# One table set for logarithm and exponential, shorter warm runs and a moved product in a two-layer transformer trunk

## What is computed

```python
for layer in range(2):
    mod = silu(c) @ ada_w[layer] + ada_b[layer]
    sh1, sc1, g1, sh2, sc2, g2 = split(mod, 6)
    h = rmsnorm(x, norm_g[layer, 0]) * (1 + sc1) + sh1
    y = diff_attention(h, ...) if layer == 0 else conformer_conv(h, ...)
    x = x + g1 * y
    h = rmsnorm(x, norm_g[layer, 1]) * (1 + sc2) + sh2
    x = x + g2 * conv_ffn(h, ...)
return rmsnorm(x, final_g)

def diff_attention(h, ...):      # per head: two softmaxes, subtracted
    p = softmax(q1 k1 + bias) - lam * softmax(q2 k2 + bias)
    o = rmsnorm(p @ v, subln_g) * (1 - lambda_init)
def conformer_conv(h, ...):
    a = glu(h @ w_pw1 + b); a = causal_dwconv(a, w_dw) + b_dw   # 31 taps
    return silu(layernorm(a)) @ w_pw2 + b_pw2
```

## Time and profile before

| | us |
|---|---|
| median of 3 runs | 1267.98 |
| the 3 runs | 1267.55, 1267.98, 1268.33 |
| the profiled execution, its own time | 1265.96 |
| span of its trace | 1264.2 |
| PE busy in the span | 1231.0 |
| DVE busy | 702.3 |
| ACT busy | 567.5 |
| POOL busy | 540.8 |

### The profile page before, as it was taken

How to read it: one execution, slowest core, us unless ns; L and a number is a source line. 1 busy time by engine, 2 the same in 40 slices (tenths; PEclk the granted TensorE clock), 3 DMA queues, 4 the chain that set the end, 5 groups by cost and what they waited for, 6 DMA issues and landing times.

```text
span 1264.2 us, 16847 instructions
## 1 busy us (share of the span) xinstructions
PE 1231.0 (97%) x5494; PEld 983.4 (78%) x5494; DVE 702.3 (56%) x1157; ACT 567.5 (45%) x899; POOL 540.8 (43%) x273
## 2 busy tenths in 40 slices
PE   7999999989999999999999999999999999999996
PEld 7877777667888888888888776577888888888884
DVE  5667766753766733346887899972533333340002
ACT  4366656644543344442223666762544444442221
POOL 1333322223433444444442699744344444454440
PEclk6899999999999999999998999999999999999998
DMA  9744443222456422236763222113233232232321
GB/s 360 214 151 148 146 154 133 101 100 67 149 184 199 166 90 93 92 105 230 232 244 112 83 84 67 33 34 100 67 100 100 100 100 90 93 106 95 105 78 66
DMA packets 45639, 157.04 MB, mean 124 GB/s; under 512 B 5536, under 2 KB 5792, under 8 KB 45600
## 3 DMA queue, kind: packets, MB, share of 16 engines
q1 hardware_dynamic: 44928, 156.21, 37.0%
q10 hardware_dynamic: 672, 0.34, 0.1%
HBM read 154.10 MB, written 2.42 MB: 124 GB/s over the span
## 4 chain that ended last, share of the span: by engine, by line
PE 81%; DVE 12%; issue 3%; ACT 2%; POOL 1%; DMA 1%; DVEq 0%; SPq 0%; ACTq 0%; POOLq 0%
PE psum L917 24%; PE psum L918 24%; PE psum L919 24%; DVE psum L1754 6%; PE psum L947 2%; PE psum L928 1%; DVE psum L1480 1%; DVE pt_lo L1489 1%; PE psum L951 1%; PE psum L1074 1%; DVE acc L1331 1%; DMA ada_first<-ada_w 1%; POOL acc_p L515 1%; PE psum L1101 1%; PE psum L1113 0%
## 5 line engine op out<-in xcount | busy, mean ns | idle before, releaser
L502 POOL TENSOR_TENSOR w_lo<-w_raw,w_hi 128x1024 fp32r<-128x1024 f32 (+1 forms) x192 | 455.2, 2387 | 670.6 <-ACT w_hi L589 670.6
L917 PE MATMUL psum<-h_hi,w_hi 128*128 128x512 f32 x1152 | 465.9, 404 | 4.1 <-DVE x L1584 2.2
L918 PE MATMUL psum<-h_lo,w_hi 128*128 128x512 f32 x1152 | 452.5, 393 | 0.0
L919 PE MATMUL psum<-h_hi,w_lo 128*128 128x512 f32 x1152 | 452.1, 392 | 0.0
L917 PEld LDWEIGHTS psum<-h_hi,w_hi 128*128 128x128 f32 x1152 | 219.0, 190 | 54.3 <-issue 7.2
L919 PEld LDWEIGHTS psum<-h_hi,w_lo 128*128 128x128 f32 x1152 | 218.5, 190 | 46.9
L918 PEld LDWEIGHTS psum<-h_lo,w_hi 128*128 128x128 f32 x1152 | 218.7, 190 | 45.6 <-issue 3.4
L589 ACT ACTIVATE w_hi<-w_raw 128x1024 fp32r<-128x1024 f32 (+1 forms) x192 | 195.6, 1032 | 82.7 <-DMA w_raw<-w_tiles 82.6
L917 PE MATMUL psum<-a_hi,w_hi 128*128 128x512 f32 x352 | 137.1, 390 | 1.0 <-issue 1.0
L919 PE MATMUL psum<-a_hi,w_lo 128*128 128x512 f32 x352 | 137.0, 389 | 0.0
L918 PE MATMUL psum<-a_lo,w_hi 128*128 128x512 f32 x352 | 136.9, 389 | 0.0
(11 more groups left out here) (185 smaller groups left out, 1342.7 us busy)
## 6 DMA issues: line engine op xcount, KB each, us to landing
w_raw<-w_tiles SPq DMA_DIRECT2D x160, 512.0 KB, 3.4
ada_buf<-ada_w SPq DMA_DIRECT2D x32, 512.0 KB, 3.4
w_raw<-w_tiles SPq DMA_DIRECT2D x32, 448.0 KB, 3.2
ada_late<-ada_w SPq DMA_DIRECT2D x28, 512.0 KB, 5.2
ada_mid<-ada_w SPq DMA_DIRECT2D x20, 512.0 KB, 4.5
ada_first<-ada_w SPq DMA_DIRECT2D x16, 512.0 KB, 10.1
x<-x_in SPq DMA_DIRECT2D x4, 512.0 KB, 7.0
bias<-rel_scratch SPq DMA_DIRECT2D x8, 256.0 KB, 6.1
```

Of the source, the lines that this page charges most:

```text
L502: nc.gpsimd.tensor_tensor(w_lo[:, slot, 0:k], w_raw[:, (ph.tile + l) % 2, 0:k], f(w_hi[:, slot, 0:k]), ALU.subtract).then_inc(lo_done, 1)
L917: nc.tensor.matmul(dst, w_hi[:, slot, k], rhs_hi, start=first, stop=False)
L918: nc.tensor.matmul(dst, w_hi[:, slot, k], rhs_lo, start=False, stop=False)
L919: return nc.tensor.matmul(dst, w_lo[:, slot, k], rhs_hi, start=False, stop=last)
```

## The change

The last of the seven late modulation sums gets its own buffer `acc_last` (in the place of `pad_g`), its product moves from ahead of PW1 to the end of the layer norm's sums, into another PSUM bank, and `late_out` is split in two calls.

```diff
--- before.py
+++ after.py
@@ -86,6 +86,7 @@
 DOWN1 = UP1.after(3, DK)
 HEAD_FROM_2 = Phase(2, 6, 3, HEADS - 2)
 PW1_FROM_2 = Phase(PW1.group + 2, PW1.tile + 4, 2, DK - 2)
+LN_EXP_SET = 6
 LATE0 = 4 + 8 * HEADS
 SQ_ORDER = (4, 5, 0, 1, 2, 3, 6, 7)
 EARLY = 4
@@ -229,7 +230,8 @@
         ada_mid = at("ada_mid", [P, 2, 2, S], F32, a_lo_at + 4 * S * 2 * MID)
         acc_mid = at("acc_mid", [P, S], F32, a_lo_at + 4 * S * (2 * MID + 4))
         ada_late = at("ada_late", [P, 4, 2, S], F32, h_base)
-        acc_late = at("acc_late", [P, LATE, S], F32, h_base + 4 * 2 * S * 4)
+        acc_late = at("acc_late", [P, LATE - 1, S], F32, h_base + 4 * 2 * S * 4)
+        acc_last = at("acc_last", [P, S], F32, offset_of["pad_g"])
 
         cursor[0] = big
         u_pad = sb("u_pad", [P, 2, TAPS - 1 + S])
@@ -255,6 +257,7 @@
         ACC_B, ACC_A, TAPS_PE, SHIFT_AT = 4, 5, 6, 7
         SUM_AT, SQ_AT = 0, 1
         DELTA_AT, RSTD_AT, SILU_AT = 4, 5, 6
+        LAST_OUT = 2
 
 
         params_in, consts_in = sem("params_in"), sem("consts_in")
@@ -598,9 +601,18 @@
                     split_tile(ph, i, ph.per_group * c + j)
 
 
+            def load_ln_exp():
+
+                nc.scalar.add_instruction(mybir.InstLoadActFuncSet(
+                    name=nc.get_next_instruction_name(), engine=mybir.EngineType.Activation,
+                    act_func_set_id=LN_EXP_SET, ins=[], outs=[]))
+
             def load_table(function):
 
-                nc.scalar.activation(sm(TABLE), ones[:, 0:1], function)
+                if function == ACT.Ln:
+                    load_ln_exp()
+                else:
+                    nc.scalar.activation(sm(TABLE), ones[:, 0:1], function)
 
             def inverse_rms(n):
 
@@ -747,7 +759,6 @@
                     copy_v(it, c + 1)
                 for m in range(EARLY if isinstance(it, int) and c == 0 else 0):
                     o_high(m)
-                load_table(ACT.Ln)
                 act.wait_ge(ms_done, lin(it, c + 1, 2))
                 nc.scalar.activation(o_sq[:], psum[:, OB], ACT.Ln, bias=sm(EPS5),
                                      scale=1.0 / (2 * HD)).then_inc(ms_read, 1)
@@ -1196,7 +1207,7 @@
 
             pairs(OUT, None, x_done, 0, 2)
             square_sum(1, 2)
-            keep_warm(18)
+            keep_warm(12)
 
             def late_ada(total, first, n):
 
@@ -1227,11 +1238,14 @@
             def last_ada(q):
 
                 pe.wait_ge(ada_used, 8 * (LATE_CH + q + 1))
-                ada_product(WARM, acc_late[:, q], at_=4 * q)
+                if q < LATE - 1:
+                    ada_product(WARM, acc_late[:, q], at_=4 * q)
+                else:
+                    ada_product(LAST_OUT, acc_last[:])
 
             last_ada(0)
             square_sum(2, 1)
-            for q in range(1, LATE):
+            for q in range(1, LATE - 1):
                 last_ada(q)
 
             def pe_taps(t):
@@ -1286,10 +1300,11 @@
             pe_taps(DK - 1)
             for n in range(4, DK):
                 dev_sums(n)
-            keep_warm(24)
+            last_ada(LATE - 1)
+            keep_warm(16)
             pairs(PW2, 4 * DK, x_done, 2 * DK, 2)
             square_sum(3, 2)
-            keep_warm(18)
+            keep_warm(12)
             pairs(UP1, 5 * DK, act_ready, FM, 1)
             group = down(DOWN1, 1)
             with pe.Fori(1, DOWN1.bodies) as i:
@@ -1400,7 +1415,7 @@
                                                in1=psum[:, OB],
                                                op0=ALU.mult, op1=ALU.mult).then_inc(t_ready, 1)
                     if m > lo:
-                        if n == 2 and m <= LATE:
+                        if n == 2 and m < LATE:
                             dve.wait_ge(ada_mm, LATE_CH + m)
                         dve.wait_ge(h_hi_ready, HI_AT[n] + m)
                         V.scalar_tensor_tensor(out=h_lo[:, m - 1], in0=turn(n, m - 1),
@@ -1605,13 +1620,13 @@
                 ab = prm[:, b4:b4 + 4] if isinstance(n, int) else prm[:, bass.ds(b4, 4)]
                 V.tensor_tensor(to, psum[:, 4, 0:4], ab, ALU.add).then_inc(sc_read, 1)
 
-            def late_out():
-
-                dve.wait_ge(ada_mm, LATE_CH + LATE)
-                first, b = 4 * LATE_CH, PARAMS["ada_b"] + 4 * LATE_CH
-                V.tensor_tensor(mod[:, first:first + 4 * LATE], psum[:, WARM, 0:4 * LATE], prm[:, b:b + 4 * LATE],
+            def late_out(lo, hi, sums):
+
+                dve.wait_ge(ada_mm, LATE_CH + hi)
+                first, b = 4 * LATE_CH + 4 * lo, PARAMS["ada_b"] + 4 * LATE_CH + 4 * lo
+                V.tensor_tensor(mod[:, first:first + 4 * (hi - lo)], sums, prm[:, b:b + 4 * (hi - lo)],
                                 ALU.add).then_inc(sc_read, 1)
-                dve.wait_ge(sc_read, LATE0 + MID + 1)
+                dve.wait_ge(sc_read, LATE0 + MID + (1 if hi < LATE else 2))
 
             def up(layer):
 
@@ -1679,7 +1694,8 @@
                     dve.wait_ge(ada_late_landed[q % 4], lin(i, 16 * (c + 1), 32))
                     for kk in range(2):
                         k = 2 * (q % 4) + kk
-                        ada_part(ada_late[:, q % 4, kk], k, tile_of(acc_late, lin(i, c, 2)),
+                        total = acc_last[:] if isinstance(i, int) else tile_of(acc_late, lin(i, c, 2))
+                        ada_part(ada_late[:, q % 4, kk], k, total,
                                  lin(i, 8 * (LATE_CH + c) + k, 16))
 
             def down0(i):
@@ -1694,7 +1710,7 @@
                 down0(i)
             down0(DOWN0.bodies - 1)
             norm(2)
-            late_out()
+            late_out(0, LATE - 1, psum[:, WARM, 0:4 * (LATE - 1)])
             V.tensor_tensor(gated_bias[:], mod[:, GATE[2]:GATE[2] + DK],
                             prm[:, PARAMS["b_pw2"]:PARAMS["b_pw2"] + DK], ALU.mult).then_inc(dve_step, own.tick())
             dve.wait_ge(dve_step, own.now())
@@ -1777,6 +1793,7 @@
             dve.wait_ge(dve_step, own.now())
             V.scalar_tensor_tensor(out=rstd[:], in0=psum[:, SQ_AT], scalar=1.0 / D, in1=rstd[:],
                                    op0=ALU.mult, op1=ALU.subtract).then_inc(var_ready, 1)
+            late_out(LATE - 1, LATE, psum[:, LAST_OUT, 0:4])
             dve.wait_ge(delta_copied, 1)
             for m in range(DK // 2):
                 V.tensor_tensor(y[:, m], y[:, m], psum[:, DELTA_AT], ALU.subtract).then_inc(dve_step, own.tick())
```

## The result

| us | before | after |
|---|---|---|
| median of the runs of this comparison | 1267.76 (1266.04 to 1268.33, 4 runs) | 1258.82 (1256.40 to 1258.89, 4 runs) |
| profiled execution | 1265.96 | 1258.75 |
| span of its trace, granted clock | 1264.2, 0.976 | 1256.9, 0.976 |

The ratio is 0.9927, with a 95% interval of 0.991 to 0.9944: faster by 0.7%. A second comparison of the same two kernels on another occasion gave 0.9942, 0.9924 to 0.996 (medians 1264.27 and 1256.64).

The account below looks back on a forecast made before the run. PE, busy 97%, was taken as the bound, so ACT savings count only where PE waits. Terms 3.7 + 2.0 + 1.1 + 1.25 + 2.0 + 1.3 = 11.35 took 1267.98 to 1256.6, range 1253.8 to 1259.0.

Parts of the forecast that it names:

- the last head stays blocked: Rival, last head: POOL again ahead of DVE's modulation sum, gain about 1.1 instead of 3.7, time 1259.2; 12%.
- Last head: Last attention head: table loads gone, buffer waits gone and third transpose earlier; gain 3.7, between 3.05 and 4.55.
- Without the delay the last head should look like this: Last head: modulation sum not delayed by POOL, third transpose at 258.55 instead of 261.62, 3.05 earlier.
- DVE is freed by more than ACT: Last head: argument against the blocked-head rival, that the change frees DVE by more than ACT.
- Norms 1 and 3: Norms 1 and 3: earlier h_lo and six fewer warm rounds become level; gain 2.0 each, between 1.9 and 2.0.
- Norm 4: Norm 4: nothing lies beside the removed table load, so its whole 1.3 is gained.
- Norm 2 and the moved product: Norm 2: four of 24 one-column products leave, 1.16; gain taken as 1.1, range -0.3 to 2.9 by the clock.
- Layer norm: Layer norm: load before Exp goes, h_lo 0.7 earlier and late next; gain 1.25, between 1.1 and 1.4.
- The shorter warm runs cost clock: Rival: one half-clock stretch behind each of norm 1, layer norm and norm 3, 5.1 in all, time 1261.7; 8%.
- ACT in the loop: Heads 0 to 6: ACT loses 2.8 a head, costed at nothing; rival that ACT bounds them, 1237.2, 3%.
- POOL ahead in every head: Rival, loop over the heads: POOL's w_lo starts before the sum in all heads, 13 slower, 1281; 3%.
- The drain of the Trainium skill, 1252.4: Table switches on the open path: a 1.38 us drain beside the 1.28 each would give an estimate of 1252.4.

Follow-up runs that it names:

- second profile with the product back: Changed kernel with the last modulation sum's product and its addition back ahead of the convolution, run a second time: median of 6 1258.20.
- three kernels with a shorter last head: Changed kernel with ACT's fourth w_hi later (1253.42), with modulation sums and weight splits moved later (1250.17), and the latter with 22 layer-norm warm rounds (1249.94).
- Only the warm runs: Kernel before the change with 12, 16 and 12 warm rounds in place of 18, 24 and 18, nothing else: ratio 0.9996.
- four extra switches: Changed kernel with four more alternating table loads between Ln and Exp of norm 4: sum of squares to final scaling 9.32 us instead of 4.18.

## Why the prediction was right in its range and wrong in its centre

The measured 1258.8 lies in the range, 2.2 above the forecast of 1256.6. But what happened is the first rival, "the last head stays blocked", which had 12% and gave 1259.2. That the number still lies in the forecast's own range is partly luck: the median before stood 2.02 above its profile and the one after 0.07, so the medians fell by more than the traces did. The sum of terms is the better test, 11.35 against 7.48 measured from mark to mark, which is below even its low end of 8.95:

- **Last head, 3.7 booked, 0.64 found.** The step that failed is "Without the delay the last head should look like this". It took for granted that the sum would be ahead of POOL's `w_lo`, because "DVE is freed by more than ACT". It was not: DVE stood waiting for scores from a PE at the low clock, and both moved by 1.3. The margin was 0.17 before and 0.19 after. The second profile with the product back confirms it: there PE had the full clock at this place and DVE did not wait, the first transpose of the last head came 1.4 earlier still, and `w_lo` again began 0.17 before the sum. When that race is turned by itself, 2.9 more is gained. In the second profile of the changed kernel the first residual comes at 186.41, which would be 1.36 for this term; the difference lies in the low-clock stretch behind the wait, 3.4 us long there and 6.8 in the first.
- **Norms 1 and 3, 2.0 each, found 1.88 and 1.85.** Right in mechanism: only both edits together pay. The forecast that loop and `h_lo` are level was off by the size of a round. It was priced by the mean, 6.04/18 = 0.336; the six left out were worth (6.04 - 3.71)/6 = 0.39. So the loop ended first, and `h_lo` decides; PE starts 0.15 behind it, not within the 0.1 that was named as a sign.
- **Norm 4, 1.3, found 1.28.** The load's row is the price, and four more of them confirm it.
- **Norm 2 and the moved product, 1.1 in a range of -0.3 to 2.9, found 0.83** in the first profile. The products themselves gave their four places, but the ones left ran slower. The wide range was right: over the four stages the same move gave 0.5 and 3.8 in two pairs. Nearly its upper end came too: in the three kernels with a shorter last head norm 2 took 6.21 to 6.24, 2.4 less than before, with a low-clock stretch of 3.4 us behind it instead of 6.8. So what this stage gives hangs on where that stretch falls.
- **Layer norm, 1.25, found 1.07.** `h_lo` was late next, as said; it came 0.61 earlier where 0.7 was forecast, and PE started 0.15 behind it and not 0.05. The small addition took 0.15. But the loop did not leave PE waiting 0.3 but 2.0, and two sizes were wrong. Eight rounds are worth 8.72 - 5.60 = 3.1, by the 16 rounds of "Only the warm runs", not 2.7. And the moved product, booked at 1.16 ahead of the loop, cost nothing there: behind it the same 16 rounds took 4.67 (with the product back, 5.52 and 5.61), so that the loop's end, 6.34 behind the last deviation sums, is not later than the 6.46 without it.
- **"The shorter warm runs cost clock", 8%,** did not happen in the first profile, and yet is true in part. Of the nine profiles here with 16 rounds, five show the second pointwise stage 1.4 to 2.5 longer (45.1 to 46.2 instead of 43.65 to 43.75), the changed kernel's second one among them. Of the four with 22 or 24 rounds none does. The wait of PE ahead of the stage does not sort them: 1.7 to 2.5 us where it is longer, 2.0 to 2.1 where it is not. Nine and four are few, but the rival deserved more than 8% (and a clock that falls behind a shortened loop was a sign named for the forecast being wrong), and for the layer norm alone: behind norms 1 and 3 the stage kept its length in every profile with 12 rounds. The argument against it, that the layer norm "leaves 0.3", rested on the two wrong sizes above.
- **ACT in the loop, cost nothing:** confirmed, the heads kept their 25.84 us without the loads. **POOL ahead in every head:** did not happen. **The drain of the Trainium skill, 1252.4:** refuted by the four extra switches.
- **Slips in the working,** too small to matter: 7 times 2.8 is 19.6 and not 19.4, three drains of 1.38 are 4.14 and not 4.2, and a distance read as 4.8 enters the sum as 4.85.

## What to carry to other kernels

When two instructions on two engines slow each other, look at who releases each of them, not at how much work was taken from either. Here both sides were let go by PE, so their order survived a saving of 2.6 us on ACT, and moving one of the two instructions changed it. A saving in front of a point where two things must be ready is worth the margin to the second, so price such edits as a pair; at norm 1 they were worth 0 and 0.6 alone and 1.9 together. A loop that only fills a wait is free up to the end of the wait; here cutting it further gained nothing and could cost clock, so cut it to that point, not below.

## What the runs showed of the hardware that was not expected

- A round of the same warm loop has no single price, even at the full granted clock. In every loop of 12 rounds or more the first products start 0.11 us apart, and the later ones 0.17 (now and then up to 0.25) and 0.21 in turn, so a round of two costs 0.22 at first and 0.39 later. The first kind are 11 to 13 products, but 21 in the changed layer norm, where the moved product stands ahead. The windows of PE there, counting the loop's products alone:

```profile
828.00:829.00 1.00, 1.00 (x11) 1.00 0.86 315
829.00:830.00 1.00, 1.00 (x8) 1.00 0.37 148
830.00:831.00 1.00, 1.00 (x6) 1.00 0.00 0
```

The rows don't say why the early ones are closer, but they show that the later price is the one that counts for rounds that are added to such a loop or left out.
- The same kernel, in two executions, had the low clock behind the layer norm once and once not, with the same PE wait of 2.04 and 2.05. Of the second, PE's windows:

```profile
831.00:833.00 2.00, 1.70 (x5) 0.64 0.00 0
833.00:835.00 2.00, 2.00 (x6) 0.51 0.00 0
```

So a single profile can't tell whether a pause of 2 us is safe. What decides it in a given execution stays open.
